# Six reduction steps of the odd mixer's first output slab placed inside the latent-attention head loop of TensorE

## The chip, the cores and the metric

The kernel runs on one core of a Trainium2 chip. The core has a matrix engine (TensorE, "PE" in the profile; its weight loads are "PEld"), a vector engine (VectorE, "DVE"), a scalar engine (ScalarE, "ACT"), a general engine (GpSimd, "POOL") and a queue engine (SyncE, "SP") that issues DMAs. Each engine works through its own list of instructions in order; semaphores tie the lists together. The metric is the device time of one execution in microseconds (us), lower is better.

## What is computed

Two transformer blocks of two layers each, on 512 tokens of width 1024, all in float32. The change touches only the last mixer, the odd one of the second block. It has eight heads of dilated attention and four heads of latent attention, whose outputs are put side by side and multiplied by one matrix `w_out`:

```python
def mla_attention(q_nope, q_rope, k_nope, k_rope, v):
    s = (einsum('bhqd,bhkd->bhqk', qn, k_nope)
         + einsum('bhqd,bkd->bhqk', qr, k_rope)).astype(float32) * scale
    s = where(qpos[:, None] >= kpos[None, :], s, NEG)
    p = softmax(s, axis=-1).astype(v.dtype)
    return einsum('bhqk,bhkd->bhqd', p, v)

def odd_mixer(h, w_in, q_norm, w_uq, kv_norm, w_ukv, w_out, rel_table):
    ...
    o_c = dilated_attention(...)          # 8 heads x 64 = rows 0 to 511 of w_out
    o_d = mla_attention(...)              # 4 heads x 128 = rows 512 to 1023
    return concatenate([merge_heads(o_c), merge_heads(o_d)], axis=-1) @ w_out
```

After it come the residual sum and the last feed-forward layer ("c1" in the code).

## The kernel before

Activations lie transposed: 128 channels on the partitions, 512 tokens along the free dimension, so 1024 channels are eight such chunks. A weight matrix comes in slabs of 256 output channels (1 MB each). A product in float32 is made of three products in the format fp32r. A slab is loaded by the SP queue into one of three `raw` buffers; ScalarE copies it, rounded, to `whi` (`act_slab`, line 200), VectorE writes the difference to `wlo` (`dve_slab`, line 211), and TensorE multiplies whi by activation-high, wlo by activation-high and whi by activation-low (`mm3`). There are two pairs `whi`/`wlo`, used in turn by the slabs. `act_slab` and `dve_slab` have fixed places in the lists of their engines: whatever stands ahead of them there must have been done.

`pe_tiles` is a generator for one slab: it first waits for `wlo` of that slab, then works through the eight chunks k of the reduction, and yields between them. One such step is 6 products of 128x512 (two blocks of output channels, three products each). `run(...)` takes all steps in one go; `next(...)` takes one. The matmul is issued in `mm`, line 218, for every product of the kernel, so line 218 alone tells little; the operands do: `ps<-R,whi` is the output product of a mixer (its activations lie in `R`), `ps<-whi,R` is the making of latent values, `ps<-F` (and `F,sacc`, `F,rs`) are scores and values of attention, `ps<-cst,F` at line 1304 is a transpose of attention weights.

Latent attention on TensorE (`pe_mla`) goes as follows. After the latent projections and the scores of heads 0 and 1 comes `pe_mla_up(1)`, which makes queries, keys and values of heads 2 and 3. Its last four groups of products are the values; ScalarE moves them out of PSUM (signals `mv`, line 1869), VectorE moves the keys out (`kn`, line 1939). Then the loop over the four heads: `pe_turn` (ten transposes, in groups of 4, 3, 2 and 1, through two PSUM banks; ScalarE copies groups of 4 and 2 out at line 1321, VectorE those of 3 and 1 at line 1316; the group of 2 waits for ScalarE's copy of the group of 4, the single one for VectorE's copy of the group of 3), then, for heads 0 and 1, the scores of head h + 2 (8 products), then `pe_values` (4 products), which waits for all four copies. The output of a head goes out through `act_out` (line 1350) and `dve_out` (line 1355), which write its high and low part as chunk 4 + h of the mixer's output (signal `o_lo_dve`).

The order on the other engines at this place is written out by hand too. ScalarE: the values of `pe_mla_up(1)`, then for each head its two copies of transposes, for heads 0 and 1 the exponentials of head h + 2, and `act_out`; after the last `act_out` comes `act_mix_out`, whose first entry is the `act_slab` of slab 1 of the output product. VectorE: the key copies, `dve_slab` of slab 0 of the output product (the last line of `dve_mla_up(1)`), then for each head the two copies, the softmax work of head h + 2, `dve_out`; after the last `dve_out`, `dve_mix_out`, whose first entry is the `dve_slab` of slab 1.

The output product (`pe_mix_out`, slabs "oddo" 0 to 3 = j) follows the loop. It writes into PSUM banks given by `mix_bank`: 4, 5 for even j and 6, 7 for odd j of this mixer. Banks 2, 3, 4 hold the scores of a latent head, 5 and 6 the transposes, 7 the values product; 0 and 1 hold the last two value groups of `pe_mla_up(1)`.

Of the kernel before, what the change touches and what calls it, by code (L numbers as in the profile page):

```python
# [216 lines left out]
def mm(e, out, l, r, start=True, stop=True):  # L217
    return e.matmul(out, l, r, start=start, stop=stop, skip_group_check=True)  # L218


def mm3(e, out, lh, ll, rh, rl, start, stop):
    mm(e, out, lh, rh, start, False)
    mm(e, out, ll, rh, False, False)
    return mm(e, out, lh, rl, False, stop)


def mm3_left(e, out, lh, ll, rh, rl, start, stop):
    mm(e, out, lh, rh, start, False)
    mm(e, out, lh, rl, False, False)
    return mm(e, out, ll, rh, False, stop)  # L230


def pe_tiles(e, s, m, n, banks, src, ready):

    s.wait_ge("wlo", n)
    hi, lo = m.w(n)
    kc = hi.shape[1]
    for k in range(kc):
        ready(k)
        for c, b in enumerate(banks):  # L240
            t = mm3(e, m.ps[b][:, :], hi[:, k, c * P:(c + 1) * P], lo[:, k, c * P:(c + 1) * P], *src(k), k == 0, k == kc - 1)
            if k == kc - 1:
                t.then_inc(*s.up("tile", n, c))
        if k < kc - 1:
            yield
    s.also("tile", n, "all")
# [12 lines left out]
def run(steps):  # L259
    for _ in steps:  # L260
        pass
# [181 lines left out]
def h_ready(s, gain):  # L443

    def ready(k):
        s.wait_ge("h_lo_pool" if gain in MOD and k % 2 else "h_lo", gain, k)
    return ready
# [461 lines left out]


def mix_bank(st, j, c):
    return (0 if st == "hyb" else 4) + 2 * (j % 2) + c


def pe_mix_out(e, s, m, st, name, ready, *half):
    for j in range(4):
        if j >= 2:
            s.wait_ge("x", st, *half, 2 * j - 3)
        run(pe_tiles(e, s, m, m.at[name, j], [mix_bank(st, j, c) for c in range(2)], m.o, ready))
# [375 lines left out]
def pe_turn(e, s, m, g):  # L1295

    for c in (3, 2, 1, 0):
        if c >= 2 and g.turn_before:
            s.wait_ge("pt_act" if c == 3 else "pt_dve", *g.turn_before, c - 2)
        elif c < 2:  # L1300
            s.wait_ge("pt_act" if c == 1 else "pt_dve", *g.key, c + 2)
        s.wait_ge("weights", *g.key, c)
        for i in range(c + 1):
            t = e.transpose(m.ps[5 + (c + 1) % 2][:, i * P:(i + 1) * P], g.p(m, c)[:, i * P:(i + 1) * P], m.k("ident"))  # L1304
        t.then_inc(*s.up("turned", *g.key, c))


def pt_of(m, g):
    return (m.E[:, 2 * T:6 * T] if g.pt else m.f(A_PT, 2048)).rearrange("p (c t) -> p c t", c=4)
# [19 lines left out]
def pe_values(e, s, m, g, value, out):  # L1329
    for c in range(4):  # L1330
        s.wait_ge("pt_act" if c % 2 else "pt_dve", *g.key, c)
    pt = pt_of(m, g)
    for i in range(4):
        t = mm(e, out[:, i * P:], value(i), pt[:, i, i * P:], i == 0, i == 3)
    t.then_inc(*s.up("pv", *g.key))
# [379 lines left out]
def mla_group(h):  # L1715
    before = ("mla", h - 1) if h else None
    return Group(("mla", h), h % 2, h % 4, before, ("mla", h - 2) if h >= 2 else ("odd", 6 + h), before)


def mla_values(m, p):  # L1720
    if p == 0:
        v = m.f(M_V, 1024).rearrange("p (c n) -> p c n", c=4)
        return [v[:, c, :] for c in range(4)]
    return [a[:, 256 * c:256 * c + 256] for a in (m.sacc, m.rs) for c in range(2)]


def mla_raw(m, n):
    return m.f(A_PT + T * n)


def pe_mla(e, s, m):
    ready = h_ready(s, "c0")
    s.wait_ge("smax", "odd", 7, 0)
    run(pe_tiles(e, s, m, m.at["mlkv", 0], (2, 3), m.h, ready))
    s.wait_ge("smax", "odd", 7, 1)
    for n in range(2):
        s.wait_ge("lq_sq", n)
        t = mm(e, m.ps[4][:, :], m.k("ones"), m.tmp[n], n == 0, n == 1)
    t.then_inc(*s.up("lq_sum"))
    s.wait_ge("pt_dve", "odd", 7, 0)  # L1740
    s.wait_ge("pt_act", "odd", 7, 1)
    s.wait_ge("lk_sq")
    mm(e, m.ps[5][:, :], m.k("ones"), m.f(M_KN)).then_inc(*s.up("lk_sum"))
    s.wait_ge("lk_in", 1)
    mm(e, m.ps[6][:, :], m.k("perm"), mla_raw(m, 3)).then_inc(*s.up("kr_turn"))
    pe_mla_up(e, s, m, 0)
    for h in range(2):
        pe_mla_scores(e, s, m, h)
    pe_mla_up(e, s, m, 1)
    for h in range(4):  # L1750
        g, (p, n) = mla_group(h), divmod(h, 2)
        if h == 0:
            s.wait_ge("kn", 1, 1)
            s.wait_ge("mv", 1, 0)
        pe_turn(e, s, m, g)
        if h < 2:
            pe_mla_scores(e, s, m, h + 2)
        if h == 0:
            s.wait_ge("mv", 1, 1)
        else:  # L1760
            s.wait_ge("o_lo_dve", "odd", 3 + h)
        v = mla_values(m, p)
        for c in range(4) if n == 0 else ():
            s.wait_ge("mv", p, c)
        pe_values(e, s, m, g, lambda c: v[c][:, P * n:P * n + P], m.ps[7][:, :])


def pe_mla_scores(e, s, m, h):
    n = h % 2
    if n == 0:  # L1770
        s.wait_ge("qn", h // 2, 1)
        s.wait_ge("rope", h // 2, 2)
        s.wait_ge("kn", h // 2, 1)
        s.wait_ge("kr", 2)
    rows = slice(64 * n, 64 * n + 64)
    pe_scores(e, s, m, mla_group(h), [(m.f(M_QN + T * n), m.f(M_KN + T * n)), (m.f(M_QR)[rows, :], m.f(M_KR)[rows, :])])


def pe_mla_up(e, s, m, p):

    q, kv = m.at["mluq", p], m.at["mlukv", p]

    def ready(k):
        s.wait_ge("lq_lo", k)

    if p == 0:
        s.wait_ge("lk_in", 0)
        s.wait_ge("lk_in", 1)
        banks, turn, keys = (0, 1, 2), 3, (4, 5)
    else:  # L1790
        s.wait_ge("mv", 0, 3)
        s.wait_ge("kn", 0, 1)
        banks, turn, keys = (0, 1, 5), 6, (7, 5)
    run(pe_tiles(e, s, m, q, banks, lambda k: (m.r(16 + 2 * k), m.r(17 + 2 * k)), ready))
    s.wait_ge("rope_x", p)
    mm(e, m.ps[turn][:, :], m.k("perm"), m.tmp[1]).then_inc(*s.up("rope_turn", p))
    s.wait_ge("wlo", kv)
    s.wait_ge("lk_lo")
    hi, lo = m.w(kv)
    if p == 0:  # L1800
        s.wait_ge("lq_rs")
        s.wait_ge("lk_rs")
    for n in range(2):
        cut = slice(n * P, n * P + P)
        mm3(e, m.ps[keys[n]][:, :], hi[:, 0, cut], lo[:, 0, cut], m.r(20), m.r(21), True, True).then_inc(*s.up("tile", kv, n))
    for c, b in enumerate((6, 7, 0, 1)):
        if p == 0 and c == 0:
            s.wait_ge("kr", 0)
        elif p == 0 and c == 1:
            s.wait_ge("o_lo_dve", "odd", 3)  # L1810
        elif c == 0:
            s.wait_ge("rope", 1, 0)
        elif c == 1:
            s.wait_ge("kn", 1, 0)
        else:
            s.wait_ge("qn", p, c - 2)
        cut = slice(c * P, c * P + P)
        t = mm3_left(e, m.ps[b][:, 0:256], m.r(20)[:, cut], m.r(21)[:, cut], hi[:, 0, 256:512], lo[:, 0, 256:512], True, True)
        t.then_inc(*s.up("tile", kv, 2 + c))
    s.also("tile", kv, "all")  # L1820
# [1132 lines left out]
def pe_hybrid(e, s, m):  # L2953
    merged(delta0=pe_gdn(e, s, m, 0), delta1=pe_gdn(e, s, m, 1), stick=pe_stick(e, s, m),
           heads=pe_stick_heads(e, s, m), ada=pe_ada_chain(e, s, m), gates=pe_gdn_gates(e, s, m))
# [22 lines left out]
def hyb_ready(s, m):  # L2978
    pe_dense_free(s, m, m.at["hybo", 0])

    def ready(k):
        if k < 4:
            s.wait_ge("o_lo", "hyb", k)
        else:
            s.wait_ge("sb_lo", 2 * k - 7)
    return ready
# [54 lines left out]
def odd_ready(s):  # L3041
    def ready(k):
        s.wait_ge("o_lo_dve", "odd", k)
    return ready


def pe_all(e, s, m):
    pe_start(e, s, m)
    pe_hybrid(e, s, m)
    pe_mix_out(e, s, m, "hyb", "hybo", hyb_ready(s, m))  # L3050
    pe_ffn(e, s, m, "s0")
    pe_ret(e, s, m)
    pe_ffn(e, s, m, "s1")
    pe_h64(e, s, m, "even")
    pe_diff(e, s, m)
    pe_mix_out(e, s, m, "even", "eveno", even_ready(s))
    pe_ffn(e, s, m, "c0")
    pe_h64(e, s, m, "odd")
    pe_mla(e, s, m)
    pe_mix_out(e, s, m, "odd", "oddo", odd_ready(s))  # L3060
    pe_ffn(e, s, m, "c1")
    pe_squares(e, s, m, "c1", 3)

# [258 lines left out]
```

## Time and profile before

| | |
|---|---|
| median of 3 runs | 2931.14 us (2929.38 to 2932.77) |
| the profiled execution's own time | 2932.45 us |
| its span, first to last instruction | 2930.5 us |
| PE busy | 2807.5 us, 96% of the span |
| DVE / ACT / POOL busy | 48% / 33% / 18% |
| mean granted TensorE clock | 0.985 of full speed |

The profile shows one execution. The span leaves out 1.95 us that the execution's own time has around it. Times of rows are counted from the start of the span. The latent head loop is a stretch of some 31 us near 2480 us, and the first slab of the output product one of 11 us behind it.

### The profile page before, as it was taken

Reading aid. Unit: us, or ns where it says so; the run is one execution under the profiler, and the core shown is the slowest. Engines: PE = TensorE matmul, PEld = TensorE weight load, DVE = VectorE, ACT = ScalarE, POOL = GpSimd, SP = SyncE. Lnnn points to the kernel's source line nnn. Section 1 sums busy time; section 2 is a strip of 40 time slices with the busy share of each in tenths; the row PEclk is TensorE's granted clock in tenths of the full one; section 3 lists DMA queues with packets and bytes.
Section 4 is the critical chain, followed back from the end, with each engine's and each line's share of the span. In section 5 each row is a group of like instructions: output and inputs, shape, how many; then the busy total and the mean of one; then the engine's idle time right before and its main releaser. Section 6 shows DMA issues by size and latency. Waiting matters only on the chain.

```text
span 2930.5 us, 33330 instructions
## 1 busy us (share of the span) xinstructions
PE 2807.5 (96%) x13978; PEld 2253.0 (77%) x13978; DVE 1403.0 (48%) x2076; ACT 963.9 (33%) x1278; POOL 532.7 (18%) x414
## 2 busy tenths in 40 slices
PE   7999889999999999999999999799999998999998
PEld 4776667888888888878888877588888875788886
DVE  5644435766645333363232455555345465454353
ACT  3444443322233322243222333432222344332222
POOL 2574211100122211221001100012112100021121
PEclk9999999999999999999999999899999999999999
DMA  6322103446332222222632322122222312122321
GB/s 231 130 80 86 44 1 131 172 175 234 135 102 97 79 87 74 88 87 97 174 108 75 115 84 82 36 101 81 99 101 84 112 62 67 72 87 79 115 83 69
DMA packets 49814, 294.26 MB, mean 100 GB/s; under 512 B 6362, under 2 KB 6490, under 8 KB 23809
## 3 DMA queue, kind: packets, MB, share of 16 engines
q1 hardware_dynamic: 43632, 274.48, 26.6%
q0 software_dynamic: 4736, 15.34, 2.0%
q8 instruction: 110, 1.80, 0.3%
q10 hardware_dynamic: 1296, 2.32, 0.2%
q14 instruction: 40, 0.32, 0.0%
HBM read 283.46 MB, written 8.65 MB: 100 GB/s over the span
## 4 chain that ended last, share of the span: by engine, by line
PE 88%; DVE 5%; ACT 4%; issue 1%; DMA 1%; POOL 1%; SPq 0%; DVEq 0%
PE ps L218 87%; DVE wlo L211 1%; PE ps L1304 1%; DVE F L2241 1%; ACT whi L200 1%; ACT F L1321 0%; DMA F<-in_ada 0%; DMA raw<-in_gdn 0%; DVE F L412 0%; DVE hl L416 0%; DVE ada L460 0%; ACT F L1280 0%; ACT E L2812 0%; ACT E L2810 0%; DVE F L819 0%
## 5 line engine op out<-in xcount | busy, mean ns | idle before, releaser
L218 PE MATMUL ps<-hh,whi 128*128 128x512 f32 x2088 | 833.2, 399 | 23.6 <-ACT F L2790 10.1
L218 PE MATMUL ps<-hl,whi 128*128 128x512 f32 x2088 | 818.2, 392 | 0.0
L218 PE MATMUL ps<-hh,wlo 128*128 128x512 f32 x2088 | 817.3, 391 | 0.0
L211 DVE TENSOR_TENSOR wlo<-raw,whi 128x2048 fp32r<-128x2048 f32 (+2 forms) x235 | 495.2, 2107 | 522.1 <-ACT whi L200 521.9
L218 PE MATMUL ps<-R,whi 128*128 128x512 f32 x2080 | 649.6, 391 | 7.8 <-DVE wlo L211 2.8
L200 ACT ACTIVATE whi<-raw 128x2048 fp32r<-128x2048 f32 (+2 forms) x235 | 409.6, 1743 | 688.8 <-PE ps L218 683.3
L218 PEld LDWEIGHTS ps<-hh,whi 128*128 128x128 f32 x2088 | 395.0, 189 | 114.3 <-ACT F L2790 10.5
L218 PEld LDWEIGHTS ps<-R,whi 128*128 128x128 f32 x2080 | 390.5, 188 | 94.7 <-issue 6.9
L218 PEld LDWEIGHTS ps<-hl,whi 128*128 128x128 f32 x2088 | 394.8, 189 | 84.0
L218 PEld LDWEIGHTS ps<-hh,wlo 128*128 128x128 f32 x2088 | 395.6, 189 | 81.9 <-issue 2.6
L218 PE MATMUL ps<-R,wlo 128*128 128x512 f32 x1040 | 404.7, 389 | 0.0
L218 PEld LDWEIGHTS ps<-R,wlo 128*128 128x128 f32 x1040 | 195.3, 188 | 40.4 <-issue 0.7
L848 POOL TENSOR_TENSOR R<-F,R 128x512 fp32r<-128x512 f32 x88 | 113.7, 1292 | 591.3 <-ACT R L758 591.3
L218 PE MATMUL ps<-F 64*64 64x32 f32 (+12 forms) x1192 | 194.4, 337 | 17.4 <-ACT F L1068 2.3
L218 PEld LDWEIGHTS ps<-F 64*64 64x64 f32 (+3 forms) x1192 | 119.1, 164 | 93.3 <-issue 64.8
L218 PE MATMUL ps<-whi,hh 128*128 128x256 f32 x512 | 146.5, 286 | 4.9 <-ACT raw L2210 2.7
L218 PE MATMUL ps<-whi,hl 128*128 128x256 f32 x512 | 145.5, 284 | 0.0
L218 PE MATMUL ps<-wlo,hh 128*128 128x256 f32 x512 | 145.5, 284 | 0.0
L845 POOL TENSOR_TENSOR F<-F,rs 128x512 f32<-128x512 f32 x44 | 56.7, 1288 | 454.0 <-ACT F L745 454.0
L295 POOL TENSOR_TENSOR sacc<-sacc,tmp 128x512 f32<-128x512 f32 x45 | 79.5, 1766 | 315.1 <-ACT tmp L283 313.5
L758 ACT ACTIVATE R<-F 128x512 fp32r<-128x512 f32 x88 | 55.8, 634 | 237.9 <-DVE F L833 232.5
L833 DVE TENSOR_TENSOR F<-ps,F 128x512 f32<-128x512 f32 x86 | 59.2, 688 | 117.7 <-POOL F L845 90.9
(341 smaller groups left out, 2561.3 us busy)
## 6 DMA issues: line engine op xcount, KB each, us to landing
F<-in_ada SPq DMA_DIRECT2D x32, 1024.0 KB, 4.8
raw<-in_fs0in SPq DMA_DIRECT2D x22, 1024.0 KB, 5.7
raw<-in_fs1in SPq DMA_DIRECT2D x22, 1024.0 KB, 4.8
raw<-in_fc0in SPq DMA_DIRECT2D x22, 1024.0 KB, 4.8
raw<-in_fc1in SPq DMA_DIRECT2D x22, 1024.0 KB, 4.8
Rf<-in_ada0h SPq DMA_DIRECT2D x24, 512.0 KB, 3.5
raw<-in_fs0out SPq DMA_DIRECT2D x16, 704.0 KB, 4.4
raw<-in_fs1out SPq DMA_DIRECT2D x16, 704.0 KB, 4.2
```

The costliest lines, as they stand in the source:

```text
L200: e.activation(m.whi[n % 2][:, 0:size], m.raw[m.slot[n]][:, 0:size], ACT.Copy).then_inc(*s.up("whi", n))
L211: e.tensor_tensor(m.wlo[n % 2][:, 0:size], m.raw[m.slot[n]][:, 0:size], m.whi[n % 2][:, 0:size].bitcast(F32), SUB).then_inc(*s.up("wlo", n))
L218: return e.matmul(out, l, r, start=start, stop=stop, skip_group_check=True)
L295: e.tensor_tensor(m.sacc[:, :], m.sacc[:, :], m.tmp[(n + 1) % 2], ADD).then_inc(*s.up("sacc", st, n))
L758: e.activation(m.o(j)[0], m.f(T2 + T * (u % 2)), ACT.Copy).then_inc(*s.up("gated_hi", st, u))
L833: e.tensor_tensor(out, m.ps[b + 1][:, :], a, MUL).then_inc(*s.up("gated", st, u))
L845: e.tensor_tensor(a, a, m.rs[:, :], MUL).then_inc(*s.up("gate_rs", st, u))
L848: e.tensor_tensor(lo, m.f(T2 + T * (u % 2)), hi.bitcast(F32), SUB).then_inc(*s.up("gated_lo", st, u))
L1304: t = e.transpose(m.ps[5 + (c + 1) % 2][:, i * P:(i + 1) * P], g.p(m, c)[:, i * P:(i + 1) * P], m.k("ident"))
L2241: e.scalar_tensor_tensor(out=out[:, k:], in0=a[:, 0:T - k], scalar=w, in1=out[:, k:], op0=MUL, op1=ADD).then_inc(*s.up("conv", h, i, k))
```

## The change

Three things change in the list of TensorE; the lists of all other engines stay as they are.

1. The output product of the odd mixer uses banks 0, 1 (even j) and 2, 3 (odd j) instead of 4, 5 and 6, 7.
2. The generator of slab 0 of that product is made before the head loop, and six of its eight steps are taken inside: one ahead of the transposes of head 0 and of head 1, and one between transposes (and scores, where there are any) and the values product of each of the four heads. A wait for the last value group (`mv`, 1, 3) is put ahead of it.
3. The last two steps (k = 6 and 7) are taken after the loop, and `pe_mix_out` starts with slab 1.

```diff
 def mix_bank(st, j, c):
-    return (0 if st == "hyb" else 4) + 2 * (j % 2) + c
+    return (0 if st in ("hyb", "odd") else 4) + 2 * (j % 2) + c
 
-def pe_mix_out(e, s, m, st, name, ready, *half):
-    for j in range(4):
+def pe_mix_out(e, s, m, st, name, ready, *half, first=0):
+    for j in range(first, 4):
...
     pe_mla_up(e, s, m, 1)
+    s.wait_ge("mv", 1, 3)
+    mixed = pe_tiles(e, s, m, m.at["oddo", 0], [mix_bank("odd", 0, c) for c in range(2)], m.o, odd_ready(s))
     for h in range(4):
         g, (p, n) = mla_group(h), divmod(h, 2)
+        if h < 2:
+            next(mixed)
...
         for c in range(4) if n == 0 else ():
             s.wait_ge("mv", p, c)
+        next(mixed)
         pe_values(e, s, m, g, lambda c: v[c][:, P * n:P * n + P], m.ps[7][:, :])
+    run(mixed)
...
-    pe_mix_out(e, s, m, "odd", "oddo", odd_ready(s))
+    pe_mix_out(e, s, m, "odd", "oddo", odd_ready(s), first=1)
```

TensorE where the head loop begins, as a difference (+ is new; the rows ahead are the last value products of `pe_mla_up(1)`, the ten transposes are those of head 0, the `ps<-F` row begins the scores of head 2):

```order
 L218 MATMUL ps<-wlo,R 128x256
 L218 MATMUL ps<-whi,R 128x256
+L218 MATMUL ps<-R,whi 128x512
+L218 MATMUL ps<-R,wlo 128x512
+L218 MATMUL ps<-R,whi 128x512 x2
+L218 MATMUL ps<-R,wlo 128x512
+L218 MATMUL ps<-R,whi 128x512
 L1304 MATMUL ps<-cst,F 128x128 x10
 L218 MATMUL ps<-F 128x512 x2
```

The step k = 0, with the wait for slab 0's `wlo` that `pe_tiles` puts ahead of it, now stands between the latent values and the first transpose.

TensorE at the last head (the ten transposes of head 3, then its values product):

```order
 L1304 MATMUL ps<-cst,F 128x128 x10
+L218 MATMUL ps<-R,whi 128x512
+L218 MATMUL ps<-R,wlo 128x512
+L218 MATMUL ps<-R,whi 128x512 x2
+L218 MATMUL ps<-R,wlo 128x512
+L218 MATMUL ps<-R,whi 128x512
 L218 MATMUL ps<-F,sacc 128x512
 L218 MATMUL ps<-F,sacc 128x384
```

The step k = 5 stands where TensorE had only the wait for the copies; the same holds for k = 4 at head 2.

ScalarE behind the loop, the same before and after the change (the second copy of head 3's transposes, its output, then `whi` of slabs 1 and 2):

```order
898 L1321 ACTIVATE F<-ps 128x2x128
899 L1350 ACTIVATE R<-ps 128x512
900 L200 ACTIVATE whi<-raw 128x2048 x2
```

Nothing moved here: the preparation of slab 1 still begins behind the output of head 3, while TensorE now has two steps of slab 0 left at that point instead of eight.

## Rows read from the trace of the kernel before

**Rows 1.** The page, parts 1 and 4: busy us and shares; chain by engine.

```profile
PE 2807.5 (96%) x13978; PEld 2253.0 (77%) x13978; DVE 1403.0 (48%) x2076; ACT 963.9 (33%) x1278; POOL 532.7 (18%) x414
...
PE 88%; DVE 5%; ACT 4%; issue 1%; DMA 1%; POOL 1%; SPq 0%; DVEq 0%
```

**Rows 2.** Timeline, PE, head 0: start us, length us, instruction, count [idle before it, releaser].

```profile
2478.36 0.28 PE L218 MATMUL ps<-whi,R 128*128 128x256 f32 x1
2478.48 0.93 PE L1304 MATMUL ps<-cst,F 128*128 128x128 f32 x7
2479.85 0.44 PE L1304 MATMUL ps<-cst,F 128*128 128x128 f32 x2 [0.44 <-ACT F L1321]
2480.56 0.33 PE L1304 MATMUL ps<-cst,F 128*128 128x128 f32 x1 [0.28 <-DVE F L1316]
2480.73 0.59 PE L218 MATMUL ps<-F 128*128 128x512 f32 x1
```

**Rows 3.** Timeline, ACT and DVE, same place.

```profile
2478.32 0.74 ACT L1869 ACTIVATE rs<-ps 128x256 f32<-128x256 f32 x2
...
2477.76 2.28 DVE L211 TENSOR_TENSOR wlo<-raw,whi 128x2048 fp32r<-128x2048 f32 x1
2479.95 0.55 DVE L1316 COPY F<-ps 128x384 f32<-128x384 f32 x1
```

**Rows 4.** Timeline, DVE and PE, a place where PE waits for `wlo`.

```profile
529.65 2.29 DVE L211 TENSOR_TENSOR wlo<-raw,whi 128x2048 fp32r<-128x2048 f32 x1
...
532.08 0.47 PE L218 MATMUL ps<-hh,whi 128*128 128x512 f32 x1 [1.69 <-DVE wlo L211]
```

**Rows 5.** Timeline, PE and DVE, transposes of a dilated head, both copying engines free.

```profile
2362.09 0.93 PE L1304 MATMUL ps<-cst,F 128*128 128x128 f32 x7
...
2363.06 0.56 DVE L1316 COPY F<-ps 128x384 f32<-128x384 f32 x1
...
2363.38 0.62 PE L1304 MATMUL ps<-cst,F 128*128 128x128 f32 x3 [0.36 <-ACT F L1321]
```

**Rows 6.** Timeline, PE and DVE, heads 1, 2 and 3.

```profile
2488.76 0.93 PE L1304 MATMUL ps<-cst,F 128*128 128x128 f32 x7
...
2489.59 0.69 DVE L1355 TENSOR_TENSOR R<-ps,R 128x512 fp32r<-128x512 f32 x1
...
2490.80 0.33 PE L1304 MATMUL ps<-cst,F 128*128 128x128 f32 x1 [0.27 <-DVE F L1316]
...
2501.05 0.33 PE L1304 MATMUL ps<-cst,F 128*128 128x128 f32 x1 [0.27 <-DVE F L1316]
...
2501.97 1.74 PE L218 MATMUL ps<-F,sacc 128*128 128x512 f32 x4 [0.59 <-DVE F L1316]
...
2506.24 0.33 PE L1304 MATMUL ps<-cst,F 128*128 128x128 f32 x1 [0.27 <-DVE F L1316]
2507.00 1.74 PE L218 MATMUL ps<-F,sacc 128*128 128x512 f32 x4 [0.43 <-DVE F L1316]
```

**Rows 7.** Timeline, PE, first and last products of slab 0.

```profile
2509.15 0.47 PE L218 MATMUL ps<-R,whi 128*128 128x512 f32 x1
...
2510.39 0.63 PE L218 MATMUL ps<-R,whi 128*128 128x512 f32 x2
...
2519.93 0.61 PE L218 MATMUL ps<-R,whi 128*128 128x512 f32 x2
```

**Rows 8.** Timeline, ACT and DVE, behind the values product of head 3.

```profile
2509.43 0.60 ACT L1350 ACTIVATE R<-ps 128x512 fp32r<-128x512 f32 x1 [3.04 <-PE ps L218]
2509.93 1.91 ACT L200 ACTIVATE whi<-raw 128x2048 fp32r<-128x2048 f32 x1
2510.06 0.69 DVE L1355 TENSOR_TENSOR R<-ps,R 128x512 fp32r<-128x512 f32 x1 [3.16 <-ACT R L1350]
...
2512.32 2.29 DVE L211 TENSOR_TENSOR wlo<-raw,whi 128x2048 fp32r<-128x2048 f32 x1 [1.56 <-ACT whi L200]
```

**Rows 9.** Stretches: PE, PEld, DVE, ACT, POOL busy, granted clock, DMA share, GB/s.

```profile
1857.50:1860.00 2.50, 1.24 (x6) 0.76 (x4) 2.36 (x14) 2.36 (x9) 0.00 (x0) 1.00 0.00 0
1860.00:1862.50 2.50, 0.78 (x2) 0.30 (x2) 1.63 (x9) 1.67 (x7) 0.00 (x0) 1.00 0.00 0
1862.50:1865.00 2.50, 1.72 (x4) 1.16 (x4) 2.50 (x7) 1.32 (x2) 0.00 (x0) 0.57 0.00 0
1865.00:1867.50 2.50, 2.50 (x7) 1.95 (x6) 1.27 (x2) 1.16 (x2) 0.44 (x1) 0.50 0.00 0
1867.50:1870.00 2.50, 2.50 (x8) 1.91 (x8) 1.13 (x1) 1.27 (x1) 1.33 (x2) 0.57 0.22 28
...
2445.00:2447.50 2.50, 0.41 (x2) 0.40 (x3) 0.56 (x2) 2.41 (x4) 1.82 (x2) 1.00 0.00 0
...
2478.48:2509.15 30.67, 26.90 (x106) 14.48 (x105) 14.61 (x46) 10.99 (x29) 0.00 (x0) 1.00 0.10 35
```

**Rows 10.** Timeline, PE, the wait inside the stretch at 2445 us.

```profile
2447.09 0.47 PE L218 MATMUL ps<-R,whi 128*128 128x512 f32 x1 [2.55 <-POOL R L1950]
```

## The prediction

> **What bounds the kernel now.** I read the page first. TensorE is busy for 96% of the span and carries 88% of the chain that ended last [rows 1]; nothing else is near. So the time changes by what the change does to the moment at which TensorE gets past slab 0 of the output product, and everything behind that moves along with it: slab 1 and what follows run without a wait in the trace until well into the feed-forward part. Next I read the head loop. From its first transpose to the first product of slab 0 it takes 30.67 us with TensorE busy for 26.90 [rows 9]. The reader should see this number first: only 3.77 us are idle there, so 3.8 us, 0.13% of the kernel, is the most that filling gaps could ever bring. Then I read the timeline at three places: the start of the loop [rows 2, 3], the waits of heads 1 to 3 [rows 6], and the point where TensorE passes from the last head into the product [rows 7, 8]. At each the question is which of the other engines' results TensorE would meet earlier than before.
>
> **The steps themselves.** A step is 6 products. The first step of slab 0 begins at 2509.15. The row at 2510.39 holds its last product and the first one of the next step, the row at 2519.93 the last product of the slab and the first one of slab 1; 42 products lie between the two rows, 9.54 / 42 = 0.23 us each. So the second step begins at 2510.62, 1.47 us for a step that follows other work, and slab 1 at 2520.16, 11.01 us for the slab [rows 7]. Taken in a row, a step is 1.37 us; standing alone costs 0.1 us more. Six steps in the loop make 6 x 1.47 = 8.82 us. The price of going from transposes or float32 products into a step is measured only at this one entry; for the way back I find no extra in the rows and take nothing. If it cost as much again, it would be 0.6 us, which I keep for the upper end.
>
> **The start of the loop: a new wait.** Today the first transpose is issued at 2478.48, right behind the latent values [rows 2]. Now the step k = 0 stands ahead of it, and it needs `wlo` of slab 0. VectorE makes that from 2477.76 to 2480.04, and ScalarE has moved the last value group out by 2479.06, so the added wait for `mv` is covered by the one for `wlo` [rows 3]. Elsewhere TensorE goes on 0.14 us after the `wlo` that it waited for (529.65 + 2.29 = 531.94, then 532.08) [rows 4]. So the step begins at 2480.18 instead of 2478.48: **+1.70 us**. What is queued behind this wait are the transposes of head 0, hence all of the loop; ScalarE and VectorE then wait for those.
>
> **Copies that come in time.** The delay pays back a part. At head 0 the single transpose (the last of ten) was at 2480.56, 2.08 us behind the first, because VectorE was on `wlo` until 2480.04 and copied only from 2479.95 on [rows 2, 3]. At head 1 it was at 2490.80, 2.04 us behind 2488.76, because VectorE was first on the output of head 0 (from 2489.59 for 0.69 us) [rows 6]. Where both engines were free, the last three transposes ran in one row: started 2363.38, together 0.62, of which the last takes 0.33, so it began at 2363.67, 1.58 us behind 2362.09 [rows 5]. Head 0 now starts after `wlo` is done, and at head 1 the step k = 2 gives the two engines 1.47 us for the output of head 0. I take 0.50 and 0.46 us, **-0.96 us** together. Not less than nothing, since the copies cannot come later with respect to their transposes than now. Heads 2 and 3 have no step ahead of their transposes and stay as they are.
>
> **Waits in front of the values products.** At heads 0 and 1 the scores of the next head already stand between, and the step there covers nothing: it is pure insertion (as is the step at the top of head 1 but for the copies just counted). At head 2 the last transpose is at 2501.05 and, as at 2480.56 to 2480.73 [rows 2], 0.17 us later the engine could have gone on; the values product began at 2501.97, 0.75 us later. At head 3 the same from 2506.24 to 2507.00 gives 0.59 us [rows 6]. Both are shorter than a step, so both vanish: **-1.34 us**. The chunks that k = 4 and k = 5 need (outputs of heads 0 and 1) have been ready for several us; no wait.
>
> **Behind the loop: the tail that is given back, and the wait that takes its place.** Six steps are gone from here, so one would book 8.2 us. But slab 1 needs its own `whi` and `wlo`, and these are queued behind the output of head 3 on ScalarE and VectorE: output from 2509.43, `whi` 2509.93 to 2511.84, `wlo` 2512.32 to 2514.61 [rows 8]. That chain hangs on the values product of head 3 and moves with it, not with the steps. Counted from 2509.15, where TensorE leaves that product, slab 1 can start at 2514.61 + 0.14 = 2514.75, after 5.60 us. The two remaining steps fill some 3.1 us of this: k = 6 until 2510.62, then k = 7 waits for the low part of head 3's output (2510.75 + 0.14 = 2510.89) and ends near 2512.3. TensorE then stands for about 2.4 us. Before, slab 1 began after 11.01 us. So the tail is shortened by 11.01 - 5.60: **-5.41 us**. Who is late next: nothing; the `whi` and `wlo` of slab 2 can be started once slab 0 is done, and slab 1 gives them 11 us of cover. The DMAs for these slabs were issued long before.
>
> **The banks.** No instruction is added by that. Slab 0 needs banks 0 and 1, free with `mv` 1, 3. Slabs 1 and 3 take 2 and 3, whose scores VectorE has read long before, and the first feed-forward slab, which also writes 0 and 1, waits for a `wlo` that VectorE makes after it has read slab 2 out of them. Cost: nothing, covered by the 11 us of slab 3; without that cover it would be two residual sums.
>
> **Sum.** 1.70 + 8.82 - 0.96 - 1.34 - 5.41 = **+2.81 us**. The profiled execution would go from 2932.45 to 2935.3; it stands 1.3 us above the median of the runs shown, so I give the sum on the median: 2931.14 + 2.81 = **2933.9 us**, 0.10% slower. I call within 0.2% (5.9 us) "same", about what a measurement of this kernel can tell from no change.
>
> **Rivals.**
>
> *Interleaving works as meant (chance 0.08).* If `wlo` of slab 1 were there in time, the tail would be 3.14 us (k = 6, the short wait, k = 7) instead of 5.60, and the sum +0.35: 2931.5. If the wait at the start fell away too, it would be -1.35: 2929.8. For it speaks only that the waits at heads 2 and 3 are real; against it, that both new waits follow from fixed orders on VectorE and ScalarE, which the change leaves alone. The Trainium skill, Perfetto Trace Analysis, section on optimization strategy, says that where the most contended engine changes over time, interleaving such regimes may improve performance. No stretch here has another bound than TensorE's, so by this trace the rule has 3.8 us to find at most; by the rule alone the time would be the 2929.8 of this rival.
>
> *The clock falls (chance 0.08, ends slower).* Near 1861 us TensorE was busy for 1.24 and 0.78 us of two stretches of 2.5 us, and then the granted clock was 0.57, 0.50 and 0.57 in the next three, that is 1.2 GHz for most of 7.5 us; 2.5 x (0.43 + 0.50 + 0.43) = 3.4 us lost. Against it stands the stretch at 2445 us, with TensorE busy for 0.41 us of 2.5 a wait of 2.55 us [rows 10], and the clock still at 1.00 [rows 9]. The two new waits (1.7 and 2.4 us) are shorter than that one, and the loop keeps TensorE busier than before in between. Should the clock fall behind the longer of them, slab 1 pays the 3.4 us, and the result is +6.2: 2937.3, above the bound. It decides as soon as the clock is below 1 for 6 us or more. The Trainium skill, TensorE: Matmul & The Clock Gate, Part 4, says that transposes do not count as busy for the clock in the way of other matmuls; by that rule the ordinary products now standing between the transposes make a fall less likely in the loop, and say nothing on the wait behind it. The sum by it stays at 2933.9.
>
> *The copies do not come earlier, and steps cost on both ends (chance 0.10).* Then +2.81 + 0.96 + 0.6 = +4.4: 2935.5, still within the bound.
>
> *The forecast (chance 0.74).* 2933.9, by itself 2932.2 to 2935.6, from the 1.7 us by which the runs shown lie around their median.
>
> **How the numbers follow.** Faster by over 0.2% would need 5.9 us where 3.8 are idle: 0.02, for what I have not seen. Slower by over 0.2%: the clock rival and the upper edge of the third, 0.10. Same: 0.88. The range goes from 2931.0, which takes in the spread of the runs below the forecast and half of the first rival, to 2937.0, which leaves out most of the clock rival.
>
> **What would show it.** In the new profile: an idle time of about 1.5 us (the last value product still counts as busy for 0.2 us of the 1.70) in front of the first `ps<-R,whi`, released by VectorE line 211; no idle time in front of the values products of heads 2 and 3; the last transpose of heads 0 and 1 some 1.6 us behind the first; about 0.1 to 0.3 us of wait at k = 7 on line 1355; and an idle time of some 2.3 us, again on line 211, in front of slab 1. From the first latent values to slab 1 the stretch should be 2.8 us longer. It would be wrong if the second of these waits were absent (then `whi` or `wlo` of slab 1 was not behind head 3), if the clock in the stretch were not 1.00, or if the difference sat outside this stretch.

## The result, and the profile after

| | before | changed |
|---|---|---|
| median of 7 runs | 2931.24 us (2929.38 to 2933.44) | 2938.88 us (2934.93 to 2944.28) |
| the profiled execution, its span | 2932.45, 2930.5 | 2940.52, 2938.5 |
| mean granted clock | 0.985 | 0.982 |

The changed kernel is slower: ratio 1.0022, 95% interval 1.0013 to 1.0031, that is 3.8 to 9.1 us. The forecast was 2933.9 us, with a range from 2931.0 to 2937.0; the sign was right, the time lies above the range.

TensorE is as busy as before, and carries the chain as before [rows 1]. The page of the changed kernel, parts 1 and 4:

```profile
PE 2814.6 (96%) x13978; PEld 2257.6 (77%) x13978; DVE 1403.7 (48%) x2076; ACT 964.0 (33%) x1278; POOL 533.8 (18%) x414
...
PE 87%; DVE 5%; ACT 4%; POOL 1%; issue 1%; DMA 1%; ACTq 0%; DVEq 0%; SPq 0%; POOLq 0%
```

TensorE is busy for 7.1 us more, with the same count of products, so there is work that ran slower. About half of it (3.4 us) lies ahead of the head loop, in instructions that the change does not touch; 3.7 us lie in the stretch from the loop to the end of the output product. The waits of TensorE in the stretch 2463 to 2540 us show the two that were forecast (first line; 1.56 and 2.19 us in the timelines below), and the waits in front of the values products of heads 2 and 3, 1.0 us before, are gone (columns: who waited for whom, us in total, times, longest):

```profile
PE ps L218 <- DVE wlo L211: 3.8, 2, 2.2
PE ps L1304 <- ACT F L1321: 1.3, 4, 0.4
PE ps L218 <- DVE F L1945: 1.0, 1, 1.0
PE ps L218 <- ACT tmp L1869: 0.7, 1, 0.7
PE ps L1304 <- DVE F L1316: 0.5, 2, 0.3
```

The timeline of TensorE, changed kernel, at the start of the loop (compare [rows 2]):

```profile
2480.73 0.28 PE L218 MATMUL ps<-whi,R 128*128 128x256 f32 x1
2482.57 0.47 PE L218 MATMUL ps<-R,whi 128*128 128x512 f32 x1 [1.56 <-DVE wlo L211]
2482.88 0.52 PE L218 MATMUL ps<-R,wlo 128*128 128x512 f32 x1
2483.20 1.05 PE L218 MATMUL ps<-R,whi 128*128 128x512 f32 x2
...
2484.90 1.67 PE L1304 MATMUL ps<-cst,F 128*128 128x128 f32 x7
```

The step waits for `wlo`, as forecast. But then a pair of products takes 1.05 us, where it took 0.63 [rows 7], and seven transposes take 1.67 us, where they took 0.93. And behind the loop, timeline of the changed kernel, TensorE and VectorE:

```profile
2520.95 0.47 PE L218 MATMUL ps<-R,whi 128*128 128x512 f32 x1
...
2526.46 0.50 PE L218 MATMUL ps<-R,whi 128*128 128x512 f32 x1 [2.19 <-DVE wlo L211]
...
2528.04 1.05 PE L218 MATMUL ps<-R,whi 128*128 128x512 f32 x2
...
2521.86 0.69 DVE L1355 TENSOR_TENSOR R<-ps,R 128x512 fp32r<-128x512 f32 x1 [3.88 <-ACT R L1350]
2524.11 2.29 DVE L211 TENSOR_TENSOR wlo<-raw,whi 128x2048 fp32r<-128x2048 f32 x1 [1.56 <-ACT whi L200]
```

Again the forecast wait, on the chain of [rows 8], and again products at half speed behind it. The granted clock in stretches of 2.5 us shows the reason (columns as in [rows 9]; the clock is the third number from the end, and 0.50 means 1.2 GHz for the whole stretch):

```profile
2480.00:2482.50 2.50, 1.01 (x9) 0.81 (x7) 2.42 (x2) 1.09 (x3) 0.00 (x0) 1.00 0.00 0
2482.50:2485.00 2.50, 2.43 (x7) 1.83 (x8) 0.00 (x0) 0.00 (x0) 0.00 (x0) 0.60 0.63 177
2485.00:2487.50 2.50, 2.19 (x12) 1.59 (x11) 0.56 (x1) 0.89 (x2) 0.00 (x0) 0.72 0.58 243
...
2525.00:2527.50 2.50, 1.04 (x4) 0.89 (x5) 2.50 (x3) 1.73 (x2) 0.00 (x0) 0.97 0.23 29
2527.50:2530.00 2.50, 2.50 (x7) 1.91 (x7) 1.40 (x3) 1.92 (x4) 1.12 (x1) 0.50 0.87 315
2530.00:2532.50 2.50, 2.50 (x10) 2.00 (x10) 2.50 (x2) 0.00 (x0) 0.21 (x1) 0.84 0.18 75
```

The clock fell behind each of the two new waits. That is the rival that was given 0.08. Below, a "fall" is such a stretch of time at 1.2 GHz behind a wait.

**How the profiles are compared.** All kernels have the same instructions up to the last latent value product (the last `ps<-whi,R` row) and again from the first product of the feed-forward layer c1 (`ps<-hh,whi`) on. I cut each profile there. In the kernel before these are the rows at 2478.36 [rows 2] and

```profile
2552.80 0.39 PE L218 MATMUL ps<-hh,whi 128*128 128x512 f32 x1
```

so the stretch between is 74.44 us. Behind the second cut every one of the 14 profiles has 377.6 to 377.7 us left. Ahead of the first they have 2476.2 to 2481.6, with the same instructions: that is the spread of an execution, and it is as large as the effects looked for. A part of it is the clock, which is below 1.00 for parts of the first 460 us in every profile and not equally long (the time lost to it, added up over stretches of 2.5 us, is 27.3 to 35.9 us). But early and again2 both lose 29.0 us there and still reach the first cut 3.05 us apart, so the rest is open. The stretch between the cuts is what a change in it can alter:

| kernel | stretch, us | against before | clock in it |
|---|---|---|---|
| before | 74.44 | | 1.00 |
| changed, four profiles | 80.14, 76.89, 80.11, 76.88 | +5.70, +2.45, +5.67, +2.44 | two falls, none, two falls, none |
| banks | 74.44 | 0.00 | 1.00 |
| nofirst | 74.44 | 0.00 | 1.00 |
| early | 76.00 | +1.56 | one fall |
| moved | 77.40 | +2.96 | one fall |
| both | 72.94 | -1.50 | 1.00 |
| two | 73.10 | -1.34 | 1.00 |
| inner | 69.74 | -4.70 | 1.00 |
| waitonly, two profiles | 82.92, 75.70 | +8.48, +1.26 | one long fall, none |

### The profile page after: what moved, and what is told of

Its sections match the earlier page's. It is cut to its first block, busy times and chain, and to the rows that moved or that the text cites. A ratio compares the mean times of both kernels' runs of the same rounds, so it can differ in the third digit from the quotient of the medians.

```text
span 2938.5 us, 33330 instructions
## 1 busy us (share of the span) xinstructions
PE 2814.6 (96%) x13978; PEld 2257.6 (77%) x13978; DVE 1403.7 (48%) x2076; ACT 964.0 (33%) x1278; POOL 533.8 (18%) x414
## 4 chain that ended last, share of the span: by engine, by line
PE 87%; DVE 5%; ACT 4%; POOL 1%; issue 1%; DMA 1%; ACTq 0%; DVEq 0%; SPq 0%; POOLq 0%
PE ps L218 86%; DVE wlo L211 1%; PE ps L1304 1%; DMA Rf<-in_ada0h 1%; ACT whi L200 1%; DVE F L2247 0%; POOL Rf L2930 0%; ACT F L1321 0%; DMA x<-in_x 0%; DVE F L412 0%; POOL Rf L2927 0%; DVE hl L416 0%; DVE ada L460 0%; ACT F L1280 0%; DVE F L819 0%
```

## Experiments

**The changed kernel again** (labels again, again2, again3; no edit). Theory A: the two waits and the clock falls behind them make up the loss. Rivals: the falls are chance (B), or the loss lies ahead of the loop (C).

> The changed kernel once more, a second profile of it. Theory A (two waits on wlo, and the granted clock falls behind each): idle 1.6 and 2.2 us before the first step and before slab 1, clock under 1 in the 5 us behind each, the stretch from the first latent value to the end of slab 1's first step some 5 us longer than before, time 5 to 7 us over the kernel before. Theory B (the clock falls were chance of one execution): same waits, clock 1.00, stretch 2.8 us longer, time about 3 us over. Theory C (part of the loss lies ahead of the head loop): the first latent values begin again more than 2 us later than the 2478.4 of before, in a kernel whose instructions up to there are the same.

> The changed kernel, a third profile. Waits of 1.6 and 2.2 us on wlo as in the two before; the stretch from the last latent value to slab 1 is 2.4 us longer where the clock stays at 1.00. Theory B (falls come by chance, in a part of the executions): one or both falls, or none. If the clock were 1.00 here as in the second profile, the falls of the first would be the exception.

> The changed kernel, a fourth profile, to count how often the clock falls behind each of the two waits. Expected by the median of the runs (5 us over before, of which 2.4 are waits and steps and each fall some 1.6): one or two falls in most profiles.

Measured: 2937.89 us median of 11 runs against 2932.75, ratio 1.0017 (1.0008 to 1.0026), or 2.3 to 7.6 us. Timeline of TensorE in the second profile:

```profile
2481.56 0.28 PE L218 MATMUL ps<-whi,R 128*128 128x256 f32 x1
2483.39 0.47 PE L218 MATMUL ps<-R,whi 128*128 128x512 f32 x1 [1.56 <-DVE wlo L211]
...
2484.85 0.93 PE L1304 MATMUL ps<-cst,F 128*128 128x128 f32 x7
2486.22 0.64 PE L1304 MATMUL ps<-cst,F 128*128 128x128 f32 x3 [0.44 <-ACT F L1321]
...
2525.66 0.50 PE L218 MATMUL ps<-R,whi 128*128 128x512 f32 x1 [2.20 <-DVE wlo L211]
```

The waits are within 0.01 us those of the first profile, but no row is slow; the clock stays at 1.00 and the stretch is 2.45 us longer. Of the four profiles two have both falls (third one: 5.67 us) and two have none (fourth one: 2.44 us). So A and B are both right in part: the waits and steps cost 2.4 us in every profile, the falls 1.63 (from the last latent value to slab 1: 45.73 us against 44.10) and 1.62 us more in a part of them. As to C: against the kernel before the first cut comes 3.2 us later in the second profile, as C expected, but 1.1 us earlier in the third and fourth. It goes both ways with the same instructions, so it is taken as spread and not as a cost of the change.

**Banks.** Only the PSUM banks, in the kernel before:

```diff
-    return (0 if st == "hyb" else 4) + 2 * (j % 2) + c
+    return (0 if st in ("hyb", "odd") else 4) + 2 * (j % 2) + c
```

> The kernel before with only the PSUM banks of the odd mixer's output product changed (0 to 3 instead of 4 to 7). Theory A: no difference, 2931 us, within 0.1%. Rival D (the banks cost something, by slab 0 waiting or by colliding with the feed-forward layer): up to 4 us slower, with an idle time of TensorE at the start of slab 0 or of the feed-forward layer.

Measured: 1.0003 (0.9994 to 1.0012), stretch 74.44 us, equal to before. The banks cost nothing; rival D is out.

**Nofirst.** The changed kernel without the step ahead of head 0's transposes:

```diff
-        if h < 2:
+        if h == 1:
             next(mixed)
```

> The changed kernel without the step ahead of the transposes of head 0: five steps in the loop, three behind it. Theory A: the first wait on wlo is gone and the clock stays at 1.00 there; sum 5 x 1.47 - 0.46 - 1.34 for the loop, and a tail of 5.60 instead of 11.01, so +0.1 us, with a wait of about 1 us before slab 1 and no clock fall: 2931.3 us. Theory B (clock falls by chance): the same +0.1, but a fall may still be seen. If the wait of the step was not the cause, the time stays near 2935 or above.

Measured: 0.9998 (0.9989 to 1.0007), stretch 74.44 us: 0.00 against an expected +0.1. The wait before slab 1 is there and half as long, since three steps stand ahead of it:

```profile
2521.30 0.50 PE L218 MATMUL ps<-R,whi 128*128 128x512 f32 x1 [1.14 <-DVE wlo L211]
```

One line of code carries the 2.4 us of cost, and the runs agree: 0.9998 here and 1.0017 for the changed kernel in the same comparison, with intervals that do not meet. That no fall came in one profile proves little by itself, since two of the four of the changed kernel have none.

**Early.** The changed kernel with `whi` and `wlo` of slab 1 ahead of the outputs of heads 2 and 3 (and taken out of `act_mix_out` and `dve_mix_out`):

```diff
         act_turn(e, s, m, mla_group(h))
+        if h == 2:
+            act_slab(e, s, m, m.at["oddo", 0] + 1)
...
+        if h == 3:
+            dve_slab(e, s, m, m.at["oddo", 0] + 1)
         dve_out(e, s, m, "odd", 4 + h, ("mla", h))
```

> The changed kernel, but ScalarE makes whi of slab 1 behind its copies for head 2 and VectorE makes wlo of slab 1 behind its copies for head 3, both ahead of the outputs. Theory A: the wait before slab 1 and the clock fall behind it are gone, the first wait and its clock fall stay: +0.35 us by the sum and 1.1 for the fall seen in the stretch, 2932.6 us. Rival E (the tail is bound by something else than the order of whi and wlo): the wait of 2.2 us before slab 1 stays and the time is that of the changed kernel.

Measured: 1.0007 (0.9999 to 1.0016), 2935.72 us median against 2932.75; stretch +1.56 us with the clock down once, behind the first wait. Less the 1.63 of that fall this is -0.1, where +0.35 was expected. There is no wait before slab 1, so rival E is out: the second wait follows from the order on ScalarE and VectorE, as the prediction had it.

**Waitonly.** The kernel before with the first wait and no step:

```diff
     pe_mla_up(e, s, m, 1)
+    s.wait_ge("wlo", m.at["oddo", 0])
     for h in range(4):
```

> The kernel before with one line more: TensorE waits for wlo of slab 0 ahead of the transposes of head 0; no step is moved. This prices the first wait alone. Theory A: 1.70 us later, 0.5 given back by the copies of head 0 that now come in time, so the stretch from the first latent values to slab 1 is 1.2 us longer with the clock at 1.00, and 1.1 to 1.7 more where the clock falls behind the wait, as in two of the three profiles so far that have this wait: 2932.5 to 2935 us. Rival F (the clock falls only because steps stand behind the wait): +1.2 us and the clock stays at 1.00.

> The kernel with the wait for wlo ahead of head 0's transposes and no step moved, a second profile. In the first the clock stood at 1.2 GHz for 17 us behind the wait and the stretch came out 9.8 us longer, while the median of its runs was 0.7 us over before. If that fall is one of several outcomes of the same instructions (theory A), this profile can show the stretch 1.2 us longer with the clock at 1.00, or a short fall and 2 to 3 us; if 9.8 us is the rule for this wait, the long fall comes again.

Measured: 1.0008 (0.9999 to 1.0016). The second profile, with the clock at 1.00, gives +1.26 us (1.62 for the wait, 0.36 given back by the copies of head 0), where 1.70 - 0.50 = 1.20 was expected: the price of the first wait is settled. The rows of the wait in the two profiles:

```profile
2481.77 2.98 PE L1304 MATMUL ps<-cst,F 128*128 128x128 f32 x10 [1.47 <-DVE wlo L211]
...
2482.15 0.98 PE L1304 MATMUL ps<-cst,F 128*128 128x128 f32 x7 [1.46 <-DVE wlo L211]
```

In the first profile the clock fell behind it and stayed down:

```profile
2480.00:2482.50 2.50, 1.03 (x7) 0.83 (x6) 1.72 (x1) 0.73 (x3) 0.00 (x0) 0.71 0.00 0
2482.50:2485.00 2.50, 2.37 (x9) 1.53 (x8) 0.77 (x2) 0.98 (x2) 0.00 (x0) 0.50 0.93 282
2485.00:2487.50 2.50, 2.50 (x4) 0.50 (x2) 0.08 (x1) 0.00 (x0) 0.00 (x0) 0.50 0.35 144
...
2495.00:2497.50 2.50, 2.50 (x4) 1.17 (x4) 1.29 (x7) 0.60 (x2) 0.00 (x0) 0.50 0.00 0
2497.50:2500.00 2.50, 2.37 (x13) 1.62 (x11) 0.97 (x4) 0.86 (x2) 0.00 (x0) 0.87 0.00 0
```

Through the scores of head 2 and the values product of head 0 it stood at 1.2 GHz, and the stretch was 8.48 us longer. (The 9.8 us in the expectation above are counted from the product behind the wait near 2447 us and take in a fall there.) So a fall does not need a step behind the wait (rival F is out), and what followed one and the same wait cost nothing in one profile and 7.2 us in the other. In the changed kernel, where steps stand among the scores, it was 1.6 us each time; whether the steps shorten such a fall is not shown, with one long fall seen, in a profile in which the clock had already fallen once some 30 us earlier.

**Moved.** The changed kernel with its first step behind the scores of head 2:

```diff
-        if h < 2:
+        if h == 1:
             next(mixed)
...
         next(mixed)
+        if h == 0:
+            next(mixed)
         pe_values(...)
```

> The changed kernel with its first step put behind the scores of head 2, so that two steps stand ahead of the values product of head 0: six steps in the loop, no wait at the start, the same wait of 2.2 us before slab 1. This prices the tail alone. Theory A: against the kernel before +0.9 us by the stretch (the 2.4 seen with the clock at 1.00, less 1.7 for the first wait, less 0.1 for one entry, plus 0.5 for the wait on the last value group), with idle 2.2 us before slab 1, and 1.7 more where the clock falls behind it. Rival G (the tail wait never brings a fall by itself, only together with the first): clock 1.00 behind it.

Measured: 1.0015 (1.0006 to 1.0023), stretch +2.96 us with one fall, behind the wait of 2.2 us:

```profile
2520.00:2522.50 2.50, 2.31 (x6) 1.84 (x7) 1.79 (x4) 1.74 (x5) 0.00 (x0) 0.57 0.52 134
2522.50:2525.00 2.50, 2.50 (x10) 1.99 (x9) 2.12 (x3) 0.64 (x2) 1.32 (x1) 0.75 0.69 285
```

Less the 1.62 of a fall that is +1.3; expected was +0.9, though its own terms (2.4 - 1.7 - 0.1 + 0.5) add up to 1.1. A fall came behind the tail wait with no fall or `wlo` wait ahead of it in the stretch, so rival G is out.

**Both.** Nofirst and early together, five steps and no wait on `wlo`.

> The changed kernel without its first step and with whi and wlo of slab 1 made before the outputs of heads 2 and 3: five steps in the loop, neither wait on wlo. Theory A: 0.0 of the kernel without the first step less its wait of 1.14 us before slab 1, so -1.1 us, no clock fall: 2931.6 against the 2932.75 of before in the last comparison, same by measurement.

Measured: 0.9998 (0.9989 to 1.0007), stretch -1.50 us, clock 1.00. The direction is as expected, the size somewhat more (-1.1); it is too small for the runs to tell from nothing.

**Two.** Only the steps that stand where TensorE waited:

```diff
-    s.wait_ge("mv", 1, 3)
     mixed = pe_tiles(...)
...
-        if h < 2:
-            next(mixed)
...
-        next(mixed)
+        if h >= 2:
+            next(mixed)
         pe_values(...)
```

> Only the two steps that stand where TensorE waited, ahead of the values products of heads 2 and 3; the other six run behind the loop. No step where nothing waits, eight us of cover for wlo of slab 1, lists of the other engines as before. Theory A: 2 x 1.47 + 6 x 1.37 + 0.1 against 11.01, less 0.75 and 0.59: -1.1 us, clock 1.00, no wait on wlo. Rival H (any step between transposes costs more than it covers): 0 or above.

Measured: 0.9999 (0.9991 to 1.0008), stretch -1.34 us (expected -1.1), clock 1.00. By the stretch, two steps with no change to the other engines do better than six (+2.45). The runs can't tell the two-step kernel from the kernel before. Rival H is out for this place.

**Inner.** Steps inside the turns, where TensorE waits for copies, and ahead of the values products of heads 2 and 3, with `whi` and `wlo` of slab 1 made as in early:

```diff
-def pe_turn(e, s, m, g):
+def pe_turn(e, s, m, g, between=None):
     for c in (3, 2, 1, 0):
+        if c == 1 and between is not None:
+            next(between)
...
-        if h < 2:
-            next(mixed)
-        pe_turn(e, s, m, g)
+        pe_turn(e, s, m, g, mixed if h else None)
...
-        next(mixed)
+        if h >= 2:
+            next(mixed)
```

> Steps where TensorE waits for copies: between the second and the third group of transposes of heads 1, 2 and 3 and ahead of the values products of heads 2 and 3, five steps; whi and wlo of slab 1 made before the outputs of heads 2 and 3. Theory A: inside a turn the waits of 0.41 and 0.27 us go, at the price of 0.1 for the entry, three times; 0.75 and 0.59 go ahead of the values products: 3 x (0.68 - 0.1) + 1.34 - 0.2 = 2.9 us less than the kernel before by the stretch, clock 1.00, 2930 us, which a measurement can hardly tell from no change. Rival H (steps between transposes cost more than they cover): 0 or above.

Measured: 2930.18 us median of 11 runs against 2933.70, ratio 0.9983 (0.9974 to 0.9992): faster than the kernel before by 2.3 to 7.6 us, and the only version here with an interval clear of 1 on that side. The stretch is 4.70 us shorter, with the clock at 1.00; 2.9 was expected. Timeline of TensorE, head 1 in inner (against 2488.76 to 2490.97 in [rows 6] and the row that follows it):

```profile
2491.29 0.93 PE L1308 MATMUL ps<-cst,F 128*128 128x128 f32 x7
2491.97 0.48 PE L218 MATMUL ps<-R,whi 128*128 128x512 f32 x1
...
2493.45 0.49 PE L1308 MATMUL ps<-cst,F 128*128 128x128 f32 x3
2493.78 8.20 PE L218 MATMUL ps<-F 128*128 128x512 f32 x24
```

The step is issued 0.68 us behind the first transpose. The kernel before went on at 2490.10, 1.34 us behind it:

```profile
2490.10 0.44 PE L1304 MATMUL ps<-cst,F 128*128 128x128 f32 x2 [0.41 <-ACT F L1321]
...
2490.97 0.59 PE L218 MATMUL ps<-F 128*128 128x512 f32 x1
```

That is 0.66 us in which nothing was issued, where the row says 0.41 of idle time: idle time is counted from the end of the last product, and the next one could have been issued before that end (in a row of products one is issued every 0.23 us while each lasts 0.39 or more). The whole turn takes 2.49 us with a step in it and took 2.21 without: 0.28 us for a step that costs 1.37 elsewhere, 1.09 saved, where 0.58 was expected. The whole loop (first transpose to first product behind it, 2480.99 to 2513.76) takes 32.77 us with five steps in it, against 30.67 without: 2.10 us for steps that cost 5 x 1.37 = 6.85 in a row.

## Why the prediction was wrong

**The first wait: right.** +1.70 us was forecast. Second profile: 1.83 us from the last value product to the step, 0.12 before to the first transpose [rows 2], so +1.71.

**The steps and what they cover: somewhat too dear.** 8.82 - 1.34 = 7.48 us were forecast, the second profile has 6.89. The two steps ahead of transposes (k = 0 and the one at the top of head 1) took 1.46 each, as forecast. The four ahead of values products cost less, 1.30 to 1.39: at head 1, for example, scores, step and values take 9.43 us (2499.31 to 2508.74) against 8.04 (2490.97 to 2499.01), 1.39 for the step. So taking the entry of [rows 7] for every step was too much by about 0.6 us in all. The way back into float32 products, kept at 0.6 us for the upper end, costs nothing.

**The copies: right, a little less.** Forecast -0.96. The turn of head 0 takes 1.84 us (2484.85 to 2486.69) instead of 2.25, that of head 1 1.82 instead of 2.21: -0.80.

**The tail: right.** Forecast -5.41: slab 1 begins 5.51 us behind the first step after the loop (2520.95 to 2526.46; the same in the second profile) instead of 11.01, -5.50, with the wait of 2.2 us on line 211 that was named. The short wait at k = 7 is there too: the row at 2521.38 of the second profile, which holds its first product, takes 0.92 us for two products instead of 0.63.

**The sum: 0.4 us off.** 1.71 + 6.89 - 0.80 - 5.50 = +2.30, and 0.15 more inside the slabs that follow, makes the 2.45 of the second profile; +2.81 was forecast. This was the expected mechanism, at about the expected size, in all four profiles of the changed kernel.

**The clock: here it failed.** The step that failed is the one that put the clock at nothing in the sum: the two new waits are shorter than the one of 2.55 us at 2445 us [rows 10], behind which the clock stayed at 1.00 [rows 9], so a fall was unlikely (0.08). What the runs showed in its place: behind the two new waits, 1.56 and 2.2 us long, the clock fell in two of four profiles of the changed kernel, for 1.6 us each, 3.25 us together. The length of a wait does not rank the risk. The wait of 2.55 us stands in all 14 profiles, and a fall followed it in only one, the first of waitonly,

```profile
2445.00:2447.50 2.50, 0.05 (x1) 0.08 (x1) 0.89 (x2) 2.14 (x4) 1.46 (x2) 0.89 0.00 0
2447.50:2450.00 2.50, 2.50 (x6) 2.02 (x7) 2.17 (x3) 1.17 (x3) 1.21 (x2) 0.50 0.03 7
```

while behind the shorter wait at the start of the loop (about 1.5 us) it fell in four of the seven profiles that have it, and behind the one of 2.2 us before slab 1 in three of five (early and moved have one wait each and fell once; the second profile of waitonly did not fall). The six profiles without a `wlo` wait of 1.4 us or more (before, banks, nofirst, both, two, inner) have no fall in the stretch between the cuts. So, as far as 14 profiles can show it, the falls go with these waits; why the wait at 2445 us was followed by one so much less often than the shorter ones, no run here shows. The rival itself was priced about right in sum, by luck: one fall of 3.4 us was assumed, and two of 1.6 came; with both, the stretch is 5.7 us longer, against the +6.2 of the rival. The prediction had named a clock below 1.00 in the stretch as a sign that it was wrong, and that is what came. A fall or two should have had about even odds or more; 2.81 for the waits and steps with 3.25 for two falls gives 2937.2 by itself, beyond the top of the range.

The words of the Trainium skill on transposes (TensorE: Matmul & The Clock Gate, Part 4) were used for the loop and left the waits open. The example of waits that bring the clock down that the same page of the Trainium skill gives, in its section on HAM oscillation, is of waits for DMA of several microseconds each. Here one of 1.56 us, with others of 0.7 and 1.0 us ahead of it, was followed by a fall in two of four profiles.

**The rest of the time.** The first comparison gave 7.6 us, the second 5.1 us. The stretch explains 2.4 to 5.7, by the number of falls, so the second comparison fits. In the first even both falls leave 2 us, and 2931.2 + 5.7 = 2936.9 would still have been inside the range: the falls take up all the room that the range had, and the last 2 us that carried the median over its edge are not explained. They are within the interval of that comparison (3.8 to 9.1), and no profile shows a further cause. How often the falls come was not measured: four profiles say about half, while the medians (2.7 and 5.2 us over the 2.4 of waits and steps, against 3.25 for both falls) point to more often than that.

**Interleaving as meant: no, and the ceiling was wrong.** The rival of 2929.8 us did not come, since its two conditions were not met in this kernel; the kernel both, which has neither `wlo` wait (with five steps for six), has -1.50 us in the stretch, near its -1.35. But the 3.8 us of idle time that I called the most that filling gaps could bring is no ceiling: inner took 4.70 us out of this stretch, with 3.77 idle in the loop [rows 9]. What was idle in the trace is not all that is free for issue.

## What to carry to other kernels

Before work is put into a gap of a busy engine, ask what that work itself waits for in its new place, and what the work behind it was hiding: here the step's own `wlo` let it start only 1.7 us after the point at which TensorE reached it, and six steps taken from the tail left bare the preparation of the next slab, which is tied to the last head by the order on two other engines. Put in as much as there is to wait, where the wait is (two steps did better than six), and move the preparation along before more is put in. Price a new wait on TensorE with and without a fall of the clock behind it, and do not call it safe because a longer wait elsewhere in one profile was.

## What the runs showed of the hardware that was not expected

The granted clock behind a wait differs between executions of one kernel: the same instructions with the same waits (1.56 and 2.2 us) ran at 1.00 in two profiles and fell to 1.2 GHz in two, at a cost of 1.6 us each. A longer wait of 2.55 us, some 33 us ahead of the first of them, was followed by a fall in one of 14 profiles. One fall, behind a wait of 1.5 us and with float32 scores and values following, lasted over 15 us and cost 7.2 us.

The idle time in a row of TensorE is less than the time in which it issues nothing: 0.41 against 0.66 us within a turn. A step placed there cost 0.28 us instead of 1.37.

Outside the stretch that the change touches, executions differ by up to 5.4 us (2476.2 to 2481.6 us to the first cut), and by 0.1 us behind the second cut.
